# A two-block transformer forward pass on one core: first attention woven with projection units, and part of the output projection moved

## What is computed

```python
def hybrid_layer(x, ...):
    x = x + 0.5 * swiglu(rmsnorm(x, ffn1_norm), ffn1_w_gate, ffn1_w_up, ffn1_w_down)
    h = rmsnorm(x, mix_norm) @ w_in
    (a_q, a_k, a_v, b_q, b_k, b_v, i_q, i_k, i_w, c_q, c_kv, c_kr) = split_columns(h)
    o_a = chunk_relpos_attention(a_q, a_k, a_v, a_rel_bias)            # 6 heads of 64
    o_b = dsa_attention(rope(b_q), rope(b_k), b_v, rope(i_q), rope(i_k), i_w)   # 5 heads, top-128 keys per query
    o_c = mla_attention(c_q, c_kv, c_kr, c_q_norm, c_kv_norm, c_w_uq, c_w_ukv)  # 5 heads
    x = x + jnp.concatenate([o_a, o_b, o_c], axis=-1) @ w_out
    return x + 0.5 * swiglu(rmsnorm(x, ffn2_norm), ffn2_w_gate, ffn2_w_up, ffn2_w_down)
# block 2: h = rms(x); fox attention with forget gates (16 heads), an RG-LRU, stick-breaking
# attention (16 heads), attention to 256 memory rows (4 heads); gated sum of the four branches;
# output projection; a convolved gated ffn
```

## Time and profile before

| | us |
|---|---|
| median of 3 runs (lowest, highest) | 4381.65 (4372.96, 4385.95) |
| the profiled execution | 4383.03 |
| its span, first to last instruction | 4381.4 |
| one layer's mix projection / gap / attention A | 190.1 / 7.0 / 105.1 |
| its C projections / attention C/B / output projection | 37.4 / 120.2 / 43.7 |
| block 2: memory stage / fox stage | 96.5 / 320.9 |
| mean granted TensorE clock | 0.926 of 2.4 GHz |

### The profile page before, as it was taken

How to read it: one execution, slowest core, us unless ns; L and a number is a source line. 1 busy time by engine, 2 the same in 40 slices (tenths; PEclk the granted TensorE clock), 3 DMA queues, 4 the chain that set the end, 5 groups by cost and what they waited for, 6 DMA issues and landing times.

```text
span 4381.4 us, 51384 instructions
## 1 busy us (share of the span) xinstructions
PE 4066.4 (93%) x17788; PEld 3216.0 (73%) x17788; DVE 1714.9 (39%) x2847; ACT 1505.5 (34%) x2448; POOL 369.0 (8%) x374
## 2 busy tenths in 40 slices
PE   8999978799999999967899989899999999789999
PEld 6887755588878887745688868787777668567888
DVE  3323565433323323664433234334432223534442
ACT  3222323432223223324332234435534553533331
POOL 1100011101001100011011000000100000100110
PEclk9999976799999999968799979999899999899999
DMA  3333310023323323200023324131112113222332
GB/s 102 96 97 97 82 42 20 1 82 96 96 82 91 96 96 93 76 19 20 29 82 96 96 86 112 39 83 44 39 54 72 39 44 91 58 73 76 96 98 98
DMA packets 495308, 316.51 MB, mean 72 GB/s; under 512 B 10832, under 2 KB 476368, under 8 KB 494640
## 3 DMA queue, kind: packets, MB, share of 16 engines
q1 hardware_dynamic: 490992, 302.86, 23.8%
q0 software_dynamic: 3008, 9.57, 0.7%
q10 hardware_dynamic: 1152, 2.10, 0.1%
HBM read 309.77 MB, written 4.33 MB: 72 GB/s over the span
## 4 chain that ended last, share of the span: by engine, by line
PE 68%; issue 21%; DVE 3%; ACT 3%; POOL 2%; PEld 1%; DVEq 1%; POOLq 0%; PEldq 0%; ACTq 0%
PE bank L214 19%; PE bank L216 19%; PE bank L215 19%; PE bank L256 1%; PE bank L1728 1%; PE bank L1734 1%; PE bank L1748 1%; PE bank L1737 1%; POOL h_lo L299 1%; PE bank L1028 1%; PE bank L1039 0%; PE bank L1030 0%; PE bank L1031 0%; PE bank L1149 0%; PE bank L648 0%
## 5 line engine op out<-in xcount | busy, mean ns | idle before, releaser
L214 PE MATMUL bank<-h_hi,w_hi 128*128 128x512 f32 (+3 forms) x3240 | 1297.9, 401 | 58.6 <-DVE w_lo L206 29.8
L215 PE MATMUL bank<-h_hi,w_lo 128*128 128x512 f32 (+3 forms) x3240 | 1279.0, 395 | 0.0
L216 PE MATMUL bank<-h_lo,w_hi 128*128 128x512 f32 (+3 forms) x3240 | 1277.7, 394 | 0.0
L206 DVE TENSOR_TENSOR w_lo<-w_raw,w_hi 128x1024 fp32r<-128x1024 f32 x571 | 737.7, 1292 | 1189.4 <-ACT w_hi L199 1183.4
L199 ACT ACTIVATE w_hi<-w_raw 128x1024 fp32r<-128x1024 f32 x571 | 598.4, 1049 | 596.4 <-DMA w_raw<-in_ffn_w_down 320.0
L214 PEld LDWEIGHTS bank<-h_hi,w_hi 128*128 128x128 f32 (+3 forms) x3240 | 612.1, 189 | 228.0 <-ACT lru_x L1831 31.0
L216 PEld LDWEIGHTS bank<-h_lo,w_hi 128*128 128x128 f32 (+3 forms) x3240 | 611.2, 189 | 140.5 <-issue 3.8
L215 PEld LDWEIGHTS bank<-h_hi,w_lo 128*128 128x128 f32 (+3 forms) x3240 | 612.5, 189 | 134.0 <-issue 4.6
L214 PE MATMUL bank<-g_hi,w_hi 128*128 (+1 forms) x880 | 342.3, 389 | 0.0
L215 PE MATMUL bank<-g_hi,w_lo 128*128 (+1 forms) x880 | 342.3, 389 | 0.0
L216 PE MATMUL bank<-g_lo,w_hi 128*128 (+1 forms) x880 | 342.3, 389 | 0.0
(11 more groups left out here) (382 smaller groups left out, 4404.1 us busy)
## 6 DMA issues: line engine op xcount, KB each, us to landing
w_raw<-in_w_in SPq DMA_DIRECT2D x161, 512.0 KB, 3.8
w_raw<-in_ffn_w_gate SPq DMA_DIRECT2D x88, 512.0 KB, 3.8
w_raw<-in_ffn_w_up SPq DMA_DIRECT2D x88, 512.0 KB, 3.8
w_raw<-in_ffn_w_down SPq DMA_DIRECT2D x88, 512.0 KB, 3.5
w_raw<-in_w_up SPq DMA_DIRECT2D x44, 512.0 KB, 3.7
w_raw<-in_w_branch SPq DMA_DIRECT2D x32, 512.0 KB, 3.8
w_raw<-in_w_out SPq DMA_DIRECT2D x24, 512.0 KB, 3.8
w_raw<-in_w_down SPq DMA_DIRECT2D x22, 512.0 KB, 3.5
```

What stands on the lines that cost most here:

```text
L206: dve.tensor_tensor(WL[:, slot(c), 0:w], RAW[:, slot(c), 0:w], WH[:, slot(c), 0:w].bitcast(F32), ALU.subtract).then_inc(w_lo, 1)
L214: pe.matmul(bank, wh, xh, start=start, stop=False)
L215: pe.matmul(bank, wl, xh, start=False, stop=False)
L216: return pe.matmul(bank, wh, xl, start=False, stop=stop)
```

## The change

- **Packed units.** The mix projection is 25 units: index key and index weights share one, as do the last 64 columns of b_q and b_k, and the last of b_v and the rope key. The host lays the columns out (`w_mix`). One more DMA on POOL moves 64 rows of b_k.
- **Two parts.** `first_items` (12 units) are the index parts and a_q, a_k, a_v, with three scores per item from item 5. `second_items` (13 units) are woven with attention A.
- **Woven attention A.** ACT and DVE take 16 item parts, PE 48 portions (an item's product is cut at k = 3 and k = 6) over 26 rounds. The items have one product bank (5) and one for what follows (6). DVE makes 5 selection rounds in the first part, 36 in attention A, 7 in the C projections. X is parked in DRAM by a DMA on POOL after the mix norm and loaded back by SP after attention A; its place holds the turned tiles.
- **Bias.** It comes laid out from the host, straight into place; only a 64x64 corner of the mask is added.
- **Output projection.** A's rows (384 of 1024) are loaded as 3 units of rows; PE makes 8 portions of 9 matmuls inside attention C/B, DVE adds them to X. The output stage has 8 units of 15 matmuls. hi and lo of the third row unit stand on ACT and DVE ahead of attention C/B.
- **Late places in C/B.** Three banks for turned tiles in place of two; copies four rounds after the scores, subtractions five, V's matmuls nine (before: three, three, seven).
- **Block 2.** PE takes items in three portions in the memory, fox and stick-breaking stages.

```diff
-N_MIX = 28
+N_MIX = 25
+N_FIRST = 12
...
-U_WO = U_UKV + 2
+U_WOA = U_UKV + 2
+U_WO = U_WOA + 3
...
+    first_items = (
+        [item(0, "rope", IKT[0:32, :], M=32, cos=2, computed=40),
+         item(0, "v", VB[:, :, 320:328], M=8, rows=slice(32, 40), shared=True)]
+        + [item(1 + t, "rope", IQT[:, t, :], scale=32 ** -0.5, cos=2) for t in range(2)]
+        + [item(3 + t, "copy", QA[:, t, :], scale=CHUNK ** -0.5) for t in range(3)]
+        + [item(6 + t, "copy", KA[:, t, :]) for t in range(3)]
+        + [item(9 + t, "v", VA[:, :, t * P:(t + 1) * P]) for t in range(3)])
+    second_items = (
+        [item(t, "copy", CQR[:, t, :]) for t in range(3)]
+        + [item(3 + t, "copy", CKVR[:, t, :]) for t in range(2)]
+        + [item(5 + t, "rope", QB[:, t, :], scale=0.125) for t in range(2)]
+        + [item(7 + t, "rope", KB_[:, t, :]) for t in range(2)]
+        + [item(9, "rope", QB[:, 2, :], scaled_rows=slice(0, 64))]
+        + [item(10 + t, "v", VB[:, :, t * P:(t + 1) * P]) for t in range(2)]
+        + [item(12, "v", VB[:, :, 256:320], M=64, computed=96),
+           item(12, "rope_in_place", KC[64:96, 0, :], M=96, rows=slice(64, 96), cos=2, shared=True)])
...
                 for k in range(x["kt"]):
+                        if thirds and k in (3, 6):
+                            yield
...
     def woven(n_a, n_b, a, b):
         for i in range(n_a):
-            if (i + 1) * n_b // n_a > i * n_b // n_a:
+            for _ in range((i + 1) * n_b // n_a - i * n_b // n_a):
                 next(b, None)
             next(a, None)
...
+        sp.wait_ge(hv_done, l * HEADS + 7)
+        pass_wait(sp)
+        sp.dma_start(x_flat, dram_x).then_inc(x_back, 16)
+        for k in range(3):
+            load(sp, q, U_WOA + k, RAW[:, slot(U_WOA + k), :], w_out[k * P:(k + 1) * P, :])
...
-    SC_FROM = 8
+    SC_FROM, SC_EACH = 5, 3
...
+            self.copied, self.subtracted, self.used = (TT, TT + 1, 2 * TT + 1) if late else (LAG, LAG, 2 * TT - 1)
+            self.rounds = self.used - TT + 2
...
+    WITH_PROJECTIONS = Places(lambda n, w: B[n % 2][:, 0:w], lambda m, a, b: B[2 + 2 * (m % 2)][:, a:b], 2,
...
+    IN_CB = Places(lambda n, w: B[n % 2][:, 0:w], lambda m, a, b: B[(2, 3, 6)[m % 3]][:, a:b], 3,
+                   lambda m, w: (SG[:, 0, 0:w], SG[:, 1, 0:w], TMP[:, 0:w], T[:, 0, 0:w])[m % 4], PT_CB, late=True)
...
+        pool.dma_start(BM[:, h % 2, :], A["bias"][bass.ds(l * 6 + h, 1)].rearrange("a p s -> (a p) s")
-    def bias_pe(pe, l, h):
-        pe.matmul(B[7][:, :], c_block(C_J), BI[h % 2][:, :], start=True, stop=True).then_inc(bm_mm, 1)
...
+    def a_output_pe(pe, l, q, m):
...
+        for k in range(3):
+            yh, yl = y_tile(k)
+            last = products(pe, B[(5, 7)[m % 2]][:, :], U_WOA + k, slice(m * P, (m + 1) * P), yh, yl, k == 0, k == 2)
...
+    def a_output_dve(dve, l, m):
+        dve.tensor_tensor(x_tile(m), B[(5, 7)[m % 2]][:, :], x_tile(m), ALU.add).then_inc(wa_done, 1)
...
+    IN_FIRST = Banks((5,), (6,))
+    A_ROUNDS = len(a_steps) + 2
+    OUT_SPLITS = {16: 0, 38: 1}
...
+        hi(act, q, U_WOA + 2)
...
+        def first_hook(e, s):
             score_dve(e, l * N_SC, s)
+            next_round(rounds, 1 if 8 <= s <= 12 else 0)
...
+        def hook(e, n):
+            if n % TT == 3 and n // TT + 1 < 6:
+                bias_dve(e, l, n // TT + 1)
+            next_round(rounds, 1 + n % 2)
...
-            for _ in range(0 if s < 12 or s == 28 else 3 if s < 18 else 2 if s >= 24 else 1):
-                next(rounds, None)
...
+        lo(dve, q, U_WOA + 2)
+            if n % TT == 3 and n // TT < KT:
+                a_output_dve(e, l, n // TT)
...
+        pool.wait_ge(nm_hf, l * N_T + 16)
+        pool.dma_start(dram_x, x_flat).then_inc(x_parked, 16)
...
-        attend_pe(pe, a_steps, l * N_STEPS, l * N_STEPS, l * HEADS, l * JOBS, l * 8, IN_A, hook=hook)
+        woven(A_ROUNDS, 3 * (len(second_items) + 2),
+              attend_pe_parts(pe, a_steps, l * N_STEPS, l * N_STEPS, l * HEADS, l * JOBS, l * 8, WITH_PROJECTIONS,
+                              banks=1),
+              project_pe_parts(pe, q, U_MIX + N_FIRST, second_items, l * N_ITEMS + N_I1, l * N_POSTS + N_P1,
+                               lambda k, s: hh(k), lambda k, s: hl(k), hook=second_hook, banks=IN_FIRST, thirds=True))
...
+        def out_hook(e, n):
+            if n % TT == 2 and n // TT < KT:
+                a_output_pe(e, l, q, n // TT)
...
-        out_pe(pe, q, U_WO, l * XL + 2 * KT, lambda e, k: e.wait_ge(y_lo, l * 8 + (8 + 2)))
+        out_pe(pe, q, U_WO, l * XL + 2 * KT, lambda e, k: e.wait_ge(y_lo, l * 8 + (8 + 2)),
+               [y_tile(k) for k in range(3, 8)])
...
-        woven(FOX_STEPS_AND_TAIL, len(fox_items1) + 2,
+        woven(FOX_STEPS_AND_TAIL, 3 * (len(fox_items1) + 2),
```

478 lines of the change are left out of this document (268 added, 210 removed).

## The result

The changed kernel takes 4299.99 us (median of 4 runs, 4298.81 to 4305.01) against 4382.27 for the kernel before: ratio 0.9818, interval 0.980 to 0.9835, a gain clear of the noise. The prediction was 4205 with a range of 4110 to 4290: the direction was right, the gain was 82 us where 178 were forecast, and the time lies 10 us above the range. The profiled execution has a span of 4298.3 us.

A forecast was written before the change was run, and what follows sets the result against it. TensorE, 93% busy, was taken as the bound on average, with time to win where it idles or runs at half clock; 4383.0 less 148.6 (two layers) and 30 (block 2) gave 4204.4, forecast 4205 us, range 4110 to 4290.

The forecast's parts named there:

- rival (d): Fox and woven attention A: spread matmuls keep the clock down, kernel slower, total 4509 us; chance 0.05.
- Rival (c): Attention C/B and block 2 give nothing: total 4245 us, or 4271 with C/B's lower bound; chance 0.12.
- the 35 us of half-clock work: Fox stage: half-clock work would take 35 us at full clock, so at most 35 goes; 25 taken.
- 24 scores 11: First part: TensorE's 24 index scores, priced as matmuls with starts, take 11 us.
- my 85.5: First part with entry to the next stage: 85.5 us forecast per layer.
- It is not the bound; DVE is: Woven attention A: DVE, not TensorE, sets the time; DVE's terms 136.5 us against PE's 113.
- My 160 us: Woven attention A: DVE's 136.5, 17 of waiting for ACT's copy, 6.5 for uneven rounds and tail.
- the terms of 136.5: Woven attention A: DVE's attention, selection rounds, `w_lo`, ropes, norms and smaller work, gaps included, sum to 136.5 us.
- 113 us at full clock: Woven attention A: TensorE's units, attention matmuls, norms and ropes take 113 us at full clock.
- Rival (a): Woven attention A: lockstep on one product bank behind ACT's copies, 210 to 215 us, total 4315; chance 0.11.
- I let all go: Attention C/B: late places remove all 26.4 us of TensorE's wait for `cb_turned_lo`.
- 22 less 4 forecast: Attention C/B: 72 added matmuls cost 22 us; TensorE's present busy time gets some 4 us shorter.

The follow-up runs named there:

- e4: The changed kernel with block 2's items given to TensorE whole, not in thirds; 4323.8 us, ratio 0.9847.
- e8: e1 with the first part's index scores taking turns in three PSUM banks in place of two; 4244.6 us, ratio 0.9677.
- e3: The changed kernel with 4 in place of 16 selection rounds per width, none in the woven part; 4254.7 us, ratio 0.9698.
- e11: e8 with the norms of c_q and c_kv one item later on TensorE, DVE and ACT; 4243.8 us, one run.
- e6: The changed kernel with the second items given to TensorE whole in woven attention A; 4299.4 us, one run.
- e1: The changed kernel with early places in attention C/B, as before the change, third bank kept; 4279.7 us, ratio 0.9749.
- e13: The changed kernel with three score banks and each C/B portion one step earlier, ahead of V's product, late places kept; 4263.2 us, one run.
- e16: e13 with ACT's splits of the next pair's q and k three steps sooner and POOL's order matched; 4237.7 us, ratio 0.9662.
- e14: e8 with each C/B portion one step later, directly ahead of V's product; 4247.1 us, one run.

## Why the prediction was right and wrong

**Right.** Output projection: 72 matmuls at 0.226, 16.3 forecast, 16.4 measured. Parking X and loading it back cost nothing that the traces show; the load back landed 7.7 us after its issue, where I had allowed 15. The C projections' seven rounds cost 0.6 us (1.4 in the second layer), not 4. The clock rose in the woven stages (A 0.52 to 0.85, fox 0.89 to 1.00, C/B 0.69 to 0.73) or stayed (memory, 0.92), against rival (d). Rival (c)'s 4271 counts 10 us twice and should be 4261; nothing rests on it.

**Fox, too small.** 25 forecast, 41 measured. The step took the 35 us of half-clock work as a cap and discounted it; the clock went to 1.00, TensorE's busy time fell by 31.3 us, and 9.8 of 15.7 us of idle went too. That thirds do something where the idles were 0.4 us was read off rightly: e4 gives them 17 us. By the Trainium skill's rule ("TensorE: Matmul & The Clock Gate", section "Why this matters for your kernels") they would have given nothing; the trace does not agree. In attention C/B of the changed kernel it agrees in part: the clock falls within two waits of over 4 us, but at 817.6 us also behind waits of 0.42 and 0.70. The other 24 us came with edits that I had passed over, the copy ahead of the splits on ACT or the 69th round; which of them is open. Block 2's surplus of 14 us was luck, and hid a part of the layers' shortfall in the total.

**First part, 19 us too low.** The step "24 scores 11" priced matmuls, and left out what one score waits for. Three in an item on two banks make the third wait for the relu of the first. e8 takes that away, the scores fall from 21.4 us with their idle to 10.5, and the part is 94; the remaining 9 over my 85.5 are in part a clock of 0.93 and an exit of 5.5 us where I took 3.

**Woven part, 17 us too low.** The failed step is "It is not the bound; DVE is", with a DVE busy for 85% or more and a clock above 0.9. DVE was busy 118.5 us, 67%, and the clock was 0.85. My 160 us left 41.5 beside those 118.5, for the gaps between instructions that the terms of 136.5 held and for 23.5 of waiting; DVE stood idle for 58.4. e3 shows that a round costs 0.7 us on the path (26.6/36), not 1.4, and that 150 us are left without any. On TensorE's side 113 us at full clock were 141.7 us, and its waits 35.2 more. e11 shows that a wait taken away comes back at the next engine. Rival (a) is not what happened: its sign, idle ahead of L217 for ACT's item copies, is 4 us here (the 5.9 in that row for `a_v` are the exit of the first part), and whole items on the one bank cost nothing (e6). Which waits would have to go together to shorten the part stays open.

**Attention C/B, 19 us too low.** The failed step is "I let all go". 18.0 of the 26.4 us went, but 16.1 of new waits came ahead of the scores, so that TensorE's idle time fell by 3.4 us in all. The portions' own term was near: 22 less 4 forecast, 17.7 us of busy time measured. V's product two steps later frees the parts two steps later, and POOL's lo parts came late: 12.8 us, and none in e1 with early places. I had named half-clock portions as a bound (a loss of 8 us), and the loss measured 14. What makes the stage good again is shown by e1, e13 and e16: 117.8 without the late places, 125.5 with the portions ahead of V's product, 114.6 with the splits earlier as well; most of that gain is clock.

## What to carry to other kernels

Price a moved step by what it waits for on its new neighbours, bank by bank, and not only by its own duration: 24 scores, three behind each unit, cost 10 us a layer for want of a third bank. When a wait is removed by deferring its user, list everything that the user frees, and what is behind that. Try filler matmuls ahead of the place where several waits meet: it gave 9 us with late places (e13) and nothing with early ones (e14), so the place has to be measured. Test two suspected causes together as well as apart: the earlier splits alone lost 5.8 us, and gained 10.9 with the portions moved. And when a helper is generalised, check the stages that you did not mean to change: fox got a 69th round and another order on ACT.

## What I had not expected of the hardware

The same 72 matmuls cost 1.0 us or 21.1 us in the same stage, mostly by the clock (0.72 to 0.84, or 0.74 to 0.73). In the late stage the granted clock alternated between 2.4 and 1.2 GHz in step with the heads; the fall at 817.6 us came after waits of only 0.42 and 0.70 us with small matmuls between them. And the first part, the same code in seven kernels, took 104.9 to 111.0 us: the clock was 0.94 where it took 104.9 and 0.91 where it took 109.5.
